# Two wide column chunks instead of four in a streamed top-2-of-8 expert layer, w2 rows in turn on a partition, six ring slots instead of seven

## The reference, cut to what matters

```python
def swiglu(x, w1, w3, w2):
    return (jax.nn.silu(x @ w1) * (x @ w3)) @ w2

def moe_ffn(x, w_router, b_router, w1, w3, w2):
    logits = (x @ w_router + b_router).astype(jnp.float32)
    top_v, top_i = lax.top_k(logits, TOP_K)          # TOP_K = 2
    top_w = jax.nn.softmax(top_v, axis=-1)
    gate = jnp.sum(jax.nn.one_hot(top_i, N_EXPERTS, dtype=jnp.float32) * top_w[..., None], axis=-2).astype(x.dtype)
    out = gate[..., 0:1] * swiglu(x, w1[0], w3[0], w2[0])
    for e in range(1, N_EXPERTS):
        out = out + gate[..., e:e + 1] * swiglu(x, w1[e], w3[e], w2[e])
    return out
```

## Time and profile before

| | us |
|---|---|
| median of 3 runs | 2609.4 (2607.05 to 2614.33) |
| profiled execution, own time | 2616.57 |
| its span, first to last instruction | 2614.8 |
| expert stage in it (first to last matmul of `tiled`) | 1550.3 to 2571 |
| one item in the middle of the stage (1995.33 to 2107.88) | 112.55 |
| TensorE busy in the span | 2393.3 (92%) |
| mean granted clock of TensorE | 0.958 |

### The profile page before, as it was taken

One profiled execution on the slowest core, in us unless ns is written; L12 is line 12 of the kernel. 1 busy time (PEld: TensorE's weight loads), 2 busy tenths in 40 slices (PEclk: granted clock), 3 DMA queues, 4 the chain that ended last, 5 costly groups with the idle time before them and its releaser, 6 DMA issues. The chain is left out here.

```text
span 2614.8 us, 61998 instructions
## 1 busy us (share of the span) xinstructions
PE 2393.3 (92%) x28274; PEld 1509.7 (58%) x28274; DVE 768.2 (29%) x1363; ACT 643.7 (25%) x974; POOL 584.2 (22%) x362
## 2 busy tenths in 40 slices
PE   4999898779999999698798779999999999999995
PEld 3776677547777778487577654444444444444443
DVE  2237765542222222615765430000000000000002
ACT  1243454332222222325455320100000000000001
POOL 4232542323333443234544300000000000000000
PEclk9999799889999999999799889999999999999997
DMA  7542001336435353231001289999999999999981
GB/s 252 193 161 77 3 4 36 99 130 218 161 129 177 113 181 109 65 121 41 6 4 36 66 325 390 402 400 397 398 401 402 399 397 401 398 372 387 404 348 55
DMA packets 205438, 565.77 MB, mean 216 GB/s; under 512 B 7856, under 2 KB 83008, under 8 KB 199552
## 3 DMA queue, kind: packets, MB, share of 16 engines
q1 hardware_dynamic: 193920, 528.63, 53.9%
q10 hardware_dynamic: 10112, 29.02, 3.4%
q0 software_dynamic: 1152, 4.19, 0.4%
HBM read 540.72 MB, written 21.10 MB: 215 GB/s over the span
## 5 line engine op out<-in xcount | busy, mean ns | idle before, releaser
L701 PE MATMUL bank<-arena 128*32 128x512 f32 (+1 forms) x6624 | 803.4, 557 | 5.9 <-issue 4.8
L311 POOL TENSOR_TENSOR w_lo<-arena,w_hi 128x2048 fp32r<-128x2048 f32 x78 | 354.2, 4542 | 627.0 <-ACT w_hi L305 626.9
L704 PE MATMUL bank<-arena 128*32 128x256 f32 (+1 forms) x6624 | 479.3, 361 | 0.0
L704 PEld LDWEIGHTS bank<-arena 128*32 128x32 f32 x6624 | 215.4, 110 | 435.5 <-issue 410.8
L321 PE MATMUL bank<-h_hi,w_hi 128*128 128x512 f32 (+1 forms) x1008 | 392.0, 389 | 48.1 <-DVE h_lo L1225 42.2
L322 PE MATMUL bank<-h_lo,w_hi 128*128 128x512 f32 (+1 forms) x1008 | 377.2, 374 | 0.0
L323 PE MATMUL bank<-h_hi,w_lo 128*128 128x512 f32 (+1 forms) x1008 | 377.0, 374 | 0.0
L701 PEld LDWEIGHTS bank<-arena 128*32 128x32 f32 x6624 | 208.7, 110 | 125.6 <-issue 10.7
L321 PEld LDWEIGHTS bank<-h_hi,w_hi 128*128 128x128 f32 x1008 | 195.2, 194 | 113.5 <-issue 61.9
L514 POOL DMA_INDIRECT arena<-slot_y,arena x4 | 3.8, 951 | 1028.6 <-ACTq L567 1027.7
L640 DVE TENSOR_TENSOR arena<-arena,bank 128x768 f32<-128x768 f32 (+2 forms) x45 | 31.3, 713 | 664.1 <-ACT arena L542 664.1
(11 more groups left out here) (262 smaller groups left out, 2521.5 us busy)
## 6 DMA issues: line engine op xcount, KB each, us to landing
arena<-in_moe_w_dram SPq DMA_DIRECT2D x189, 2048.0 KB, 12.2
arena<-in_w_mod_dram SPq DMA_DIRECT2D x48, 1024.0 KB, 5.0
arena<-in_ffn_w_dram SPq DMA_DIRECT2D x42, 1024.0 KB, 7.0
arena<-in_w_in_dram SPq DMA_DIRECT2D x26, 1024.0 KB, 6.3
arena<-in_w_out_dram SPq DMA_DIRECT2D x8, 1024.0 KB, 9.6
slot_x<-arena ACTq DMA_DIRECT2D x1, 4992.0 KB, 26.3
slot_y<-arena ACTq DMA_DIRECT2D x1, 4992.0 KB, 55.7
x_store<-arena ACTq DMA_DIRECT2D x2, 2048.0 KB, 6.5
```

The source lines that it names most:

```text
L311: pool.tensor_tensor(lo, slot_view(splits[i][0]), hi, ALU.subtract).then_inc(sem("w_lo"), 1)
L701: mm(bank[b][64 * h + 32 * c:64 * h + 32 * c + 32, 0:n // 2], xa[:, 32 * c:32 * c + 32], w[:, n // 2 * h:n // 2 * (h + 1)], start=first, s ...
L704: ins = mm(bank[b + 1][blk(q), 0:n // 4], xb, w[:, n // 4 * q:n // 4 * (q + 1)], start=first, stop=last)
```

## The change

The chunks become 2048 and 1536 columns wide. w1 and w3 units hold two rows of 2048 (8 KB runs, 2 MB) or two of 1536 (6 KB runs, 1.5 MB). w2 units hold four (chunk 0) or three (chunk 1) rows, and now neighbouring rows of the matrix lie in turn on one partition, `"(p k) n -> p k n"`, so that a partition gets one run of 16 or 12 KB. The pass has 24 units, and the ring six slots. `tiled` streams up to 512 columns at a time over two banks and the quarters in a third; w1 uses banks 0 to 2 and w3 banks 3 to 5. The transposed gate goes to banks 3 to 5 as well, so w3 of chunk s waits for `m_gt` of chunk s - 1. `turn` has 12 and 9 transposes in place of 6, 6, 6 and 3, reading every fourth (third) column of GSM (`block_cols`) to match the new rows of w2. GSM and the sigmoid's buffer move to the area of `HB`, GT takes their place.

```diff
-    MRING = 7
+    MRING = 6
-    CHUNKS = [(c, min(1024, FF - c)) for c in range(0, FF, 1024)]
+    CHUNKS = [(c, min(2048, FF - c)) for c in range(0, FF, 2048)]
+    W2_ROWS = (4, 3)
...
-        GSM = area(o_m, 768)
-        SGM = area(o_m + 768, 768)
-        GT = area(o_m + 1536, 6, P)
+        GSM = area(o_hb, 1536)
+        SGM = area(o_hb + 1536, 1536)
+        GT = area(o_m, 12, P)
...
             kind, s, _ = u
-            return MUNIT // (D if kind == "w2" else CHUNKS[s][1])
+            return W2_ROWS[s] if kind == "w2" else MUNIT // CHUNKS[s][1]
...
+        def block_cols(f, s):
+
+            n = W2_ROWS[s]
+            c = P * n * (f // n) + f % n
+            return slice(c, c + n * (P - 1) + 1, n)
...
-                sp.dma_start(moe_slot(j), src.rearrange("(k p) n -> p k n", p=P)) \
+                src = src.rearrange("(p k) n -> p k n" if kind == "w2" else "(k p) n -> p k n", p=P)
+                sp.dma_start(moe_slot(j), src) \
                   .then_inc(sem(f"slot{j % MRING}"), 16)
...
-                src, n = turned(4, s)
+                src, n = turned(3, s)
                 act.activation(GT[:, 0:n], src, ACT.Copy).then_inc(sem("m_gt"), 1)
...
-                for h in range(2):
-                    for c in range(2):
-                        mm(bank[b][64 * h + 32 * c:64 * h + 32 * c + 32, 0:n // 2], xa[:, 32 * c:32 * c + 32],
-                           w[:, n // 2 * h:n // 2 * (h + 1)], start=first, stop=last)
+                for c0 in range(0, n // 2, 512):
+                    nc_ = min(512, n // 2 - c0)
+                    for h in range(2):
+                        for c in range(2):
+                            mm(bank[b][64 * h + 32 * c:64 * h + 32 * c + 32, 0:nc_], xa[:, 32 * c:32 * c + 32],
+                               w[:, n // 2 * h + c0:n // 2 * h + c0 + nc_], start=first, stop=last)
+                    b += 1
                 for q in range(4):
-                    ins = mm(bank[b + 1][blk(q), 0:n // 4], xb, w[:, n // 4 * q:n // 4 * (q + 1)], start=first, stop=last)
+                    ins = mm(bank[b][blk(q), 0:n // 4], xb, w[:, n // 4 * q:n // 4 * (q + 1)], start=first, stop=last)
...
                 pe.wait_ge(sem("m_s" if kind == "w1" else "m_g"), NC * i + s + 1)
+                if kind == "w3":
+                    pe.wait_ge(sem("m_gt"), NC * i + s + 1)
...
-                dst, n = turned(4, s)
+                dst, n = turned(3, s)
                 for f in range(n):
-                    ins = nc.tensor.transpose(dst[:, f], GSM[:, f * P:(f + 1) * P], ident)
+                    ins = nc.tensor.transpose(dst[:, f], GSM[:, block_cols(f, s)], ident)
```

More of the change, by code:

```diff
@@ L445, in spans @@
             n = CHUNKS[s][1]
-            if n == 1024:
-                return [(ps[:, b:b + 2, :].rearrange("p b n -> p (b n)")[:, 0:768], slice(0, 768))]
-            return [(bank[b][:, 0:n // 2], slice(0, n // 2)), (bank[b + 1][:, 0:n // 4], slice(n // 2, n // 2 + n // 4))]
+            if n == 2048:
+                return [(ps[:, b:b + 3, :].rearrange("p b n -> p (b n)"), slice(0, 1536))]
+            return [(ps[:, b:b + 2, :].rearrange("p b n -> p (b n)")[:, 0:n // 2], slice(0, n // 2)),
+                    (bank[b + 2][:, 0:n // 4], slice(n // 2, n // 2 + n // 4))]
         def turned(b, s):
             n = CHUNKS[s][1] // 512 * 3
-            return ps[:, b:b + 2, :].rearrange("p b (f n) -> p (b f) n", n=P)[:, 0:n], n
+            return ps[:, b:b + 3, :].rearrange("p b (f n) -> p (b f) n", n=P)[:, 0:n], n
+        def block_cols(f, s):
+            n = W2_ROWS[s]
+            c = P * n * (f // n) + f % n
+            return slice(c, c + n * (P - 1) + 1, n)
         def moe_slot(j):
-            return area(o_ring + (j % MRING) * MUNIT, MUNIT).rearrange("p (k n) -> p k n", k=unit_rows(order[j]))
+            return area(o_ring + (j % MRING) * MUNIT, unit_rows(order[j]), D if order[j][0] == "w2" else CHUNKS[order[j][1]][1])
         def moe_sp(sp):
@@ L643, in item @@
                     dve.wait_ge(sem("m_s"), NC * i + s + 1 + 1)
-                    for src, cols in spans(2, s):
+                    for src, cols in spans(3, s):
                         ins = tt(GSM[:, cols], SGM[:, cols], src, ALU.mult)
@@ L716, in hidden @@
                     for r in range(unit_rows(u)):
-                        ins = tiled(0 if kind == "w1" else 2, CHUNKS[s][1], XG[:, k, 0:NS_A], XG[:, k, NS_A:SLOTS],
+                        ins = tiled(0 if kind == "w1" else 3, CHUNKS[s][1], XG[:, k, 0:NS_A], XG[:, k, NS_A:SLOTS],
                                     moe_slot(place[u])[:, r], k == 0, k == KD - 1)
```

## The result

The changed kernel is slower: median 2627.4 us (2623.2 to 2631.5, 4 runs) against 2609.1 (2607.1 to 2614.3), a ratio of 1.0066 with an interval of 1.0048 to 1.0083. The forecast was 2622.1 in a range of 2614 to 2638. Measured once more beside the experiments it was 1.0068 (1.0053 to 1.0083). One of those seven executions took 7375 us at a granted clock of 0.33 and is left out as a slow one; why it was slow is open.

What follows compares the result with a forecast made beforehand. TensorE was taken to set the expert stage's pace, transfers following. Turns add 1.7 us and calls save 0.3: 1.4 an item, 12.7 us over nine items, added to 2609.4: 2622.1 us, range 2614 to 2638.

Steps and rivals of the forecast that it cites:

- What bounds the kernel: Expert stage: TensorE sets the pace and waits for no DMA; transfers follow, with some 19 us to spare.
- First turn: Chunk 0's twelve transposes 1.54 us, then gate copy 1.45 us before w3 starts: 3.07 us, where it was 0.81.
- Second turn: Chunk 1's nine transposes 1.21 us, then copy 1.13 us before `down` starts: 2.43 us in place of 1.14.
- Calls: `tiled` calls of w1 and w3, fewer and wider: 0.3 us less an item, 0.1 as the other end.
- Strided loads: Transposes' weight loads reading every fourth or third float: taken as no cost, bounded at 2.3 us an item, 21 in all.
- strided rival: Strided weight loads of the transposes are slow: up to 21 us on top, 2643 us; chance 5%.
- The transfers: Weight DMA of the stage: same bytes, larger runs and six slots cost nothing, since nobody waits for them.
- The clock: Rival: TensorE's clock falls at the first turn, 8 to 15 us more, 2630 to 2637, up to 2645; chance 12%.
- The loop's stall: Rival: stall at the loop's way back, 7.4 us once, goes; 2614.7 us, not slower; chance 8%.
- The late transfers: Rival: smaller slots and one fewer make transfers late; at 372 GB/s 53 us more, 2662 us; chance 3%.
- the copy did hold up TensorE: Answers a rival at w3 after the first turn: copy holds up nobody, item 0.85 us less, 2601.7 us; chance 4%.
- four signs of being wrong: Clock 0.50 behind turns, twelve transposes over 1.6 us, TensorE waiting for a slot, or the loop's stall gone.

Runs made afterwards that it cites:

- plain rows: Changed kernel with w2 units again as separate 4 KB runs and transposes reading GSM without a stride: 1.0057 of before, item 114.09 us.
- the thinned kernels: TensorE doing only each unit's first row (and a chunk's last): kernel before 0.9812, wide chunks with w2 in 4 KB runs 0.9782, changed kernel 0.9726 of before.
- the run that doesn't jump: Changed kernel with both turns hidden, w2 in 4 KB runs, and item 6 written out on TensorE so its loop runs once: 2599.3 us, 0.9957 of before.
- the three kernels with the mixes of run length above: Thinned kernels, TensorE on few rows: kernel before (4 and 2 KB), wide chunks (8, 6, 4 KB), changed kernel (8, 6, 16, 12 KB): 0.9812, 0.9782, 0.9726.

## Why the prediction was right, point by point

**What bounds the kernel.** Right, and shown: half the bytes change nothing, one wait on TensorE's path changes all. The margin of the kernel before was thinner than the waits told: it asked for 399 GB/s of the 404 that came with TensorE out of the way. With runs of 4 and 2 KB, a change that took more than 1.5 us out of its item would have met the transfers.

**First turn.** Forecast 3.07 us, measured 3.30. The copy (1.45) and its start 0.04 behind the transposes were right to a hundredth. Mis-sized were two terms. The twelve transposes end after 1.72 us and not 1.54: with plain rows, and nothing else changed in the transposes, it is 1.53. And TensorE starts 0.10 after the copy, not 0.06. That 0.06 came from a second turn, and at the second turn it holds (1865.19 + 1.13 = 1866.32 to 1866.38); at the first it is 0.10, and 0.24 in the last three items. Those three are the ones whose number is held in a register (the loop and the item behind it), but that this is the reason is not shown.

**Second turn.** Forecast 2.43, measured 2.52, for the same first reason: nine transposes end after 1.30, not 1.21, and after 1.20 with plain rows.

**Calls.** I took 0.3 us of gain an item, with 0.1 as the other end. The overhead goes by instructions after all (0.015 us on 24 instead of 0.01 on 16), and the gain is 0.15.

**Strided loads.** I took nothing, with 21 us as the bound. They cost 0.29 us an item, 2.6 in all. The bound's form was right (a slower spacing), my choice of zero was not. I reasoned that the load is not what spaces the plain transposes, and that is so, but it says nothing of a load half as long again. This part of the strided rival (5%) came true, at an eighth of its bound.

**The transfers.** That they cost nothing was right. One reading behind it was not: the 2 MB in runs of 16 KB that took 6.5 us were a store to HBM; in the same profile the load of those 2 MB back took 8.8. That longer runs need less time was shown only by the thinned kernels.

**The sum.** 112.55 + 1.4 was forecast and 114.38 measured. The missing 0.43 us are 0.23 and 0.09 of the turns and 0.15 of the calls, with rounding; times nine, 3.9 us, by which the 12.7 fell short of 16.5. The rest of the median's 18.3 lies within its interval. All three misses are on the same side, so no luck made them cancel; and 2627.4 lies just above the 2618 to 2627 that I gave the forecast by itself, so that the number was right by its wide range, which was made for the rivals.

**The rivals.** The clock did not fall at the turns: 1.00 over the whole stretch. With 1.6 us of standing between twelve transposes and the next call, nine times, no fall followed. By the Trainium skill ("TensorE: Matmul & The Clock Gate", PE-mode transpose) transposes don't count as activity; the nine stretches would then have been 3.3 us of idle each, more than the 2 us that were followed by a fall in the earlier trace rows. The measurement speaks against it here. The loop's stall stayed at 4.6 us, so its rival fell; that it is the jump back was shown by the run that doesn't jump. The late transfers did not come, and the copy did hold up TensorE.

**What I said would show it.** The item, the copies (1.45 and 1.13), the calls and the gaps of 1.5 and 0.6 us (1.59 and 0.56) are there. One of my four signs of being wrong came as well: the twelve transposes took more than 1.6 us, and this is the mis-sized term above. The other three did not. The profile puts six of the nine long gaps down to "issue" and three to ScalarE. The DMA share fell under 1.0 by a hundredth only (0.99). A landing under 10 us was wrong: it is 12.1 and 9.8. I divided an item's bytes by its length. Within a chunk TensorE frees 2 MB every 5.15 us and 1.5 MB every 3.87, so the queue is asked for 407 GB/s there, close to its 416; only the turns let it catch up. With half the bytes a wide unit lands in 5 us.

## What to carry to other kernels

Where two full resources run side by side, ask the waits which one follows: work on the follower (here 3% of faster transfers) buys nothing. Then thin out the leader to see how close the follower is; here it was 1.5 us an item. When tiles are made larger to help transfers, look what shares a buffer or a bank afterwards; a copy that was free beside the next matmuls became the longest wait of the item, and moving its producer to the middle of other work gave all of it back, and more. Price such a wait as producer, hand-over, copy and release, each from its own row, and check it on several items: here the sizes repeated to a hundredth of a microsecond, but for one hand-over in the last three items.

## What the runs showed of the hardware

- A weight load of 128 x 128 floats takes 140 ns when its columns lie side by side, 212 ns at a stride of 16 bytes (a first turn) and 198 at one of 12 (a second turn); the transposes start 0.109, 0.121 and 0.115 us apart.
- Streaming from HBM into 128 partitions gave 404, 412 and 416 GB/s for the three kernels with the mixes of run length above, over 770 us, 98% of it on one queue.
- Twelve transposes and 1.6 us of idle, once an item, left TensorE's clock at 2.4 GHz (1.00) from 1560 to 2330 us; in the 4.6 us of idle at the loop's way back it fell, and it stayed at 1.2 GHz for 6.8 us, 4.7 of them behind the idle.
- Three units of lead (four slots) were enough at 392 GB/s, 94% of the 416 that such runs can give; two (three slots) were not, and cost 2.7% of the time.
